# A relative-position bias table built as eight single rows and repeated 128 times by a memory-to-memory transfer, in a two-block decoder kernel

## The reference, cut to what matters

```
score = sum_h w_idx[q,h] * relu(q_idx[q,h] . k_idx[s])      # causal
sel   = top_k(score, 128)
dist  = t[:, None] - sel
logits = q_abs @ c_kv[sel] + rel_bias[rel_bucket(dist)]     # rel_bias is [32 buckets, 8 heads]
p = masked_softmax(logits, dist >= 0)
```

## Time and profile before

| | |
|---|---|
| profiled execution, its time | 2313.94 us |
| its span | 2312.1 us |
| TensorE busy | 2268.6 us, 98% |
| VectorE / ScalarE / GpSimd busy | 1128.8 (49%) / 870.7 (38%) / 389.9 us (17%) |
| mean granted TensorE clock | 0.987 |
| chain that ended last, by engine | PE 91%, ACT 3%, DVE 3%, DMA 1%, POOL 1% |

### The profile page before, as it was taken

How to read it: one execution, slowest core, us unless ns; L and a number is a source line. 1 busy time by engine, 2 the same in 40 slices (tenths; PEclk the granted TensorE clock), 3 DMA queues, 4 the chain that set the end, 5 groups by cost and what they waited for, 6 DMA issues and landing times.

```text
span 2312.1 us, 26070 instructions
## 1 busy us (share of the span) xinstructions
PE 2268.6 (98%) x10840; PEld 1842.9 (80%) x10840; DVE 1128.8 (49%) x1728; ACT 870.7 (38%) x1291; POOL 389.9 (17%) x339
## 2 busy tenths in 40 slices
PE   7999999999999999999999999999999999999998
PEld 5567888888876678888888878888888888888887
DVE  4974433434335645344345566554333446555553
ACT  5674222223225633122134485442322344233343
POOL 1431110112200012011032303332101211000020
PEclk9799999999999999999999999999999999999999
DMA  4203322322361022322345523224255333332331
GB/s 138 101 1 110 109 91 91 101 94 96 96 189 39 1 74 92 107 93 91 98 89 92 37 37 65 46 46 83 55 92 103 98 92 91 110 91 91 100 107 58
DMA packets 221955, 196.26 MB, mean 85 GB/s; under 512 B 7264, under 2 KB 215596, under 8 KB 221709
## 3 DMA queue, kind: packets, MB, share of 16 engines
q1 hardware_dynamic: 219820, 188.92, 31.1%
q0 software_dynamic: 1504, 5.51, 0.7%
q10 hardware_dynamic: 513, 0.17, 0.0%
HBM read 189.87 MB, written 4.72 MB: 84 GB/s over the span
## 4 chain that ended last, share of the span: by engine, by line
PE 91%; ACT 3%; DVE 3%; DMA 1%; POOL 1%; issue 0%; ACTq 0%; POOLq 0%
PE bank L540 24%; PE bank L542 24%; PE bank L541 24%; PE bank L2225 5%; PE bank L863 3%; PE bank L2411 2%; PE bank L1692 1%; PE bank L847 1%; PE bank L714 1%; PE bank L724 1%; PE bank L1309 1%; PE bank L2101 1%; DVE weight_lo L526 1%; PE bank L1510 0%; DVE hybrid_step L2340 0%
## 5 line engine op out<-in xcount | busy, mean ns | idle before, releaser
L540 PE MATMUL bank<-h_hi,weight_hi 128*128 128x512 f32 (+1 forms) x1568 | 616.4, 393 | 4.7 <-DVE h_lo L646 3.6
L542 PE MATMUL bank<-h_hi,weight_lo 128*128 128x512 f32 (+1 forms) x1568 | 612.5, 391 | 0.0
L541 PE MATMUL bank<-h_lo,weight_hi 128*128 128x512 f32 (+1 forms) x1568 | 612.1, 390 | 0.0
L526 DVE TENSOR_TENSOR weight_lo<-weight_raw,weight_hi 128x2048 fp32r<-128x2048 f32 (+3 forms) x181 | 382.9, 2116 | 363.0 <-ACT weight_hi L517 362.9
L517 ACT ACTIVATE weight_hi<-weight_raw 128x2048 fp32r<-128x2048 f32 (+2 forms) x182 | 319.8, 1758 | 335.9 <-PE bank L542 312.4
L540 PEld LDWEIGHTS bank<-h_hi,weight_hi 128*128 128x128 f32 (+1 forms) x1568 | 295.0, 188 | 68.7 <-issue 7.4
L542 PEld LDWEIGHTS bank<-h_hi,weight_lo 128*128 128x128 f32 (+1 forms) x1568 | 294.7, 188 | 63.3
L541 PEld LDWEIGHTS bank<-h_lo,weight_hi 128*128 128x128 f32 (+1 forms) x1568 | 294.9, 188 | 61.7 <-issue 0.2
L540 PE MATMUL bank<-hidden_hi,weight_hi 128*128 128x512 f32 x512 | 201.8, 394 | 0.0
L542 PE MATMUL bank<-hidden_hi,weight_lo 128*128 128x512 f32 x512 | 200.7, 392 | 0.0
L541 PE MATMUL bank<-hidden_lo,weight_hi 128*128 128x512 f32 x512 | 198.7, 388 | 0.0
(11 more groups left out here) (414 smaller groups left out, 3140.8 us busy)
## 6 DMA issues: line engine op xcount, KB each, us to landing
weight_raw<-in_w_down SPq DMA_DIRECT2D x40, 1024.0 KB, 5.1
weight_raw<-in_w_up SPq DMA_DIRECT2D x32, 1024.0 KB, 5.4
weight_raw<-in_w_up SPq DMA_DIRECT2D x44, 512.0 KB, 5.0
weight_raw<-in_w_in SPq DMA_DIRECT2D x20, 1024.0 KB, 8.8
weight_raw<-in_w_in SPq DMA_DIRECT2D x24, 512.0 KB, 6.7
weight_raw<-in_w_kv_shared SPq DMA_DIRECT2D x6, 1024.0 KB, 4.9
weight_raw<-in_w_branch SPq DMA_DIRECT2D x6, 1024.0 KB, 5.0
weight_raw<-in_a_w_o SPq DMA_DIRECT2D x4, 1024.0 KB, 5.7
```

Of the source, the lines that this page charges most:

```text
L526: dve.e.tensor_tensor(split_flat(v, 1), raw_flat(v), f32(split_flat(v, 0)), ALU.subtract).then_inc(*split.mark(("unit", v)))
L540: pe.e.matmul(o, w[0], x[0], start=start, stop=False)
L541: pe.e.matmul(o, w[0], x[1], start=False, stop=False)
L542: return pe.e.matmul(o, w[1], x[0], start=False, stop=stop)
```

## The change

`rel_bias` is no longer widened. Two matmuls (33 x 8 by 33 x 320) give all heads at once, one row a partition, early in the stage, right after `sums("kidx")`. ScalarE copies them to an 8 x 640 row buffer (20 KB). GpSimd writes that to a new DRAM tensor `bias_line`, waits for it, and starts one DRAM to DRAM transfer that reads each row 128 times and fills `skew` (2.6 MB), before it adds any score. The sheared read of `skew` is issued by GpSimd between the scores of tiles 2 and 3. The 16 matmuls, their copies, the eight sends and the waits on them are gone.

```diff
+        bias_line = nc.dram_tensor("bias_line", [HEADS, N_SHIFT], F32, kind="Internal")
-        bias_rows = [dsa_step(at, N_SHIFT) for at in (6 * T, 6 * T + N_SHIFT, 0, N_SHIFT)]
-        rel_wide = dsa_step(4 * T, HEADS, P)
+        bias_row = dsa_step(4 * T, N_SHIFT)
+        BIAS_PARTS = [(0, N_SHIFT // 2), (N_SHIFT // 2, N_SHIFT)]
@@ dsa_tensor
             sums("kidx", 64)
+            pe.wait_ge(*hot_in.when("hot"))
+            pe.wait_ge(*rel_in.when("rel"))
+            pe.wait_ge(*dsa.dve.when("neg"))
+            for n, (c0, c1) in enumerate(BIAS_PARTS):
+                bank = open_bank(pe, ("bias", n), (dsa.act, ("bias", n)))
+                pe.e.matmul(bank[0:HEADS, 0:c1 - c0], rel, one_hot[:, c0:c1], start=True, stop=True
+                            ).then_inc(*dsa.pe.mark(("bias", n)))
...
-            pe.wait_ge(*dsa.act.when("rel_wide"))
-            pe.wait_ge(*hot_in.when("hot"))
-            for h in range(HEADS):
-                for half in range(2):
-                    bank = open_bank(pe, ("bias", h, half), (dsa.act, ("bias", h, half)))
-                    pe.e.matmul(bank[:, 0:w], rel_wide[0:BUCKETS + 1, h, :], one_hot[:, half * w:half * w + w], start=True,
-                                stop=True).then_inc(*dsa.pe.mark(("bias", h, half)))
@@ dsa_scalar
                              ).then_inc(*dsa.act.mark(("w_rows",), ("kidx", "taken")))
+            for n, (c0, c1) in enumerate(BIAS_PARTS):
+                act.wait_ge(*dsa.pe.when("bias", n))
+                act.e.activation(bias_row[0:HEADS, c0:c1], banks.of("bias", n)[0:HEADS, 0:c1 - c0], ACT.Copy
+                                 ).then_inc(*dsa.act.mark(("bias", n)))
             scalar_fold(act, dsa, "kidx", latent_factors["kidx"], 1.0 / IDX_DIM)
...
-            act.e.activation(rel_wide[0:BUCKETS + 1], rel.unsqueeze(2).broadcast_to([BUCKETS + 1, HEADS, P]), ACT.Copy
-                             ).then_inc(*dsa.act.mark(("rel_wide",)))
...
-            for h in range(HEADS):
-                for half in range(2):
-                    act.wait_ge(*dsa.pe.when("bias", h, half))
-                    if h > 3:
-                        act.wait_ge(*skew_out[h % 4].when("skew", h - 4))
-                    act.e.activation(bias_rows[h % 4][:, half * w:half * w + w], banks.of("bias", h, half)[:, 0:w], ACT.Copy
-                                     ).then_inc(*dsa.act.mark(("bias", h, half)))
...
-                act.wait_ge(*skew_out[1].when("skew", HEADS - 3))
...
-                else:
-                    act.wait_ge(*skew_out[h].when("skew", HEADS - 4 + h))
@@ dsa_pool
             pool_squares(pool, dsa)
+            for n in range(2):
+                pool.wait_ge(*dsa.act.when("bias", n))
+            pool.e.dma_start(bias_line[:, :], bias_row[0:HEADS]).then_inc(*skew_out.mark(("line",), by=16))
+            pool.wait_ge(*skew_out.when("line"))
+            pool.e.dma_start(skew[:, :, :], bass.AP(tensor=bias_line, offset=0, ap=[[N_SHIFT, HEADS], [0, P], [1, N_SHIFT]])
+                             ).then_inc(*skew_out.mark(("skew",), by=16))
             for i in (2, 3):
...
+                if i == 2:
+                    sheared = bass.AP(tensor=skew, offset=P - 1, ap=[[N_SHIFT - 1, P], [P * N_SHIFT, HEADS], [1, T]])
+                    pool.wait_ge(*skew_out.when("skew"))
+                    pool.e.dma_start(bias[:, :, :], sheared).then_inc(*bias_in.mark(("bias",), by=16))
             uq = unit_at["uq", 0]
             pool.wait_ge(*rounded.when("unit", uq))
             pool.e.tensor_tensor(split_flat(uq, 1), raw_flat(uq), f32(split_flat(uq, 0)), ALU.subtract
                                  ).then_inc(*dsa.pool.mark(("unit", uq)))
-            for h in range(HEADS):
-                pool.wait_ge(*dsa.act.when("bias", h, 1))
-                pool.e.dma_start(skew[h], bias_rows[h % 4]).then_inc(*skew_out[h % 4].mark(("skew", h), by=16))
-            sheared = bass.AP(tensor=skew, offset=P - 1, ap=[[N_SHIFT - 1, P], [P * N_SHIFT, HEADS], [1, T]])
-            for n in range(4):
-                pool.wait_ge(*skew_out[n].when("skew", HEADS - 4 + n))
-            pool.e.dma_start(bias[:, :, :], sheared).then_inc(*bias_in.mark(("bias",), by=16))
```

More of the change, by code:

```diff
@@ L438, in build_program @@
         raw_in = [signal(f"weight_in{n}") for n in range(2 * N_RAW)]
-        skew_out = [signal(f"skew_out{n}") for n in range(4)]
-        bias_in, misc_in, out_done = signal("bias_in"), signal("misc_in"), signal("out_done")
+        skew_out, bias_in, misc_in, out_done = (signal(n) for n in ("skew_out", "bias_in", "misc_in", "out_done"))
         tile_full, rounded, split = signal("tile_full"), signal("weight_rounded"), signal("weight_split")
@@ L1048, in dsa_tensor @@
                                 start=True, stop=True).then_inc(*dsa.pe.mark(("score", i, h)))
-            w = N_SHIFT // 2
-            pe.wait_ge(*dsa.act.when("rel_wide"))
-            pe.wait_ge(*hot_in.when("hot"))
-            for h in range(HEADS):
-                for half in range(2):
-                    bank = open_bank(pe, ("bias", h, half), (dsa.act, ("bias", h, half)))
-                    pe.e.matmul(bank[:, 0:w], rel_wide[0:BUCKETS + 1, h, :], one_hot[:, half * w:half * w + w], start=True,
-                                stop=True).then_inc(*dsa.pe.mark(("bias", h, half)))
             u = unit_at["uk", 0]
@@ L1123, in dsa_scalar @@
                 act.e.activation(q_idxT[:, t, :], banks.of("q_idx", t), ACT.Copy).then_inc(*dsa.act.mark(("q_idx", t)))
-            act.wait_ge(*dsa.dve.when("neg"))
-            act.wait_ge(*rel_in.when("rel"))
-            act.e.activation(rel_wide[0:BUCKETS + 1], rel.unsqueeze(2).broadcast_to([BUCKETS + 1, HEADS, P]), ACT.Copy
-                             ).then_inc(*dsa.act.mark(("rel_wide",)))
             n = 0
```

## The result

Measured: 2316.17 us median (2313.39 to 2318.14, 21 runs) against 2312.71 (2310.22 to 2315.45, 21 runs); ratio 1.0015, 95% interval 1.001 to 1.0021. That is 3.5 us slower where 1.4 was forecast; within 0.2%. The profiled execution has a span of 2315.4 us.

What follows compares the result with a forecast made beforehand. VectorE's unbroken 64 us key search bounds the changed stretch; its 0.54 us delay is swallowed at L754, then L764 adds 1.4: 2313.94 + 1.4 = 2315.3, forecast 2315.2 us, within 0.2% (4.6 us); middle cases 2312.0 to 2318.5.

Steps and rivals of the forecast that it cites:

- The bound: VectorE's top-128 key search, 60.68 to 124.71 us, is unbroken and ends last before the attention.
- the freed `uq` path: Ahead of the attention: `uq` product 10 us earlier, worth 0; rival that this path was last, 2305.2 us, 5%.
- over 3: Slack of the `uq` path: first logit tile done near 121.6 us, over 3 us before it is used.
- no wait for another engine in it: VectorE's search for tiles 1 to 3, 64.03 us, was taken as never waiting for another engine.
- L540 of cq "near 92": Start of the `uq` product, behind L764 and its spread: near 92 us instead of 100.85.
- Added matmuls: Two bias matmuls ahead of L1033 delay TensorE's q_idx and first score by 0.84 us, 0.3 to 1.3.
- L1126: Widening of rel_bias on ScalarE ahead of the first relu: removing it gains 0.30 us, so the search begins 0.54 late.
- GpSimd's shift: Sheared-read issue and late scores move GpSimd's L1273 by 1.4 us, 0.9 to 2.0, delaying VectorE; rival no stall, 2314.1 us, 18%.
- L764 is about 1.9 us long: Midway in VectorE's search, L764 stalls until GpSimd's L1273 ends near 90.25 us, leaving 1.4 us later.
- The clock: TensorE's half-clock restart at the attention taken as equal in both kernels, bounds -1.5 to +1.5 us.
- The repeat: DRAM to DRAM copy lands between 60 and 70 us, holding nobody; late rivals 2317.9 us, 8%, and 2385, 4%.

Runs made afterwards that it cites:

- short-search pair: Kernel before and changed kernel, each with 8 instead of 16 key-search rounds for query tile 3: 2309.67 and 2302.99 us.
- a_again: The changed kernel run again with no edit: 2315.46 us against 2312.34 for the kernel before, ratio 1.0011.
- SyncE's share: Changed kernel with all three bias transfers issued by SyncE instead of GpSimd: 2315.39 us; with the bias matmuls also moved between q_idx tiles: 2314.27 us.
- the last variant: Changed kernel with bias matmuls behind tile 1's scores, transfers on SyncE, no extra tensor, fold on ScalarE, last scale step after tile 2's search: 2310.17 us.

## Why the prediction was right, and where its sizes were off

- **The bound** was right: no other engine opens a gap on VectorE in the search, and the short-search pair shows that the freed `uq` path is worth 0 until the search shrinks. Its slack was 2.7 us, not "over 3". And "no wait for another engine in it" holds for gaps alone: some 1.3 us of the search were GpSimd's hold inside L754 and L764 (1.17 and 0.48 us, where each takes 0.16 alone).
- **L540 of cq "near 92".** 92.48 in a_again and 94.63 in the first trace, in both 1.8 us after the end of L764 (90.64 and 92.78): the mechanism as told.
- **Added matmuls, "I take 0.84".** Measured 2.15 - 1.28 = 0.87 (L1041 in a_again against L1033). Right.
- **L1126, "0.30 us gained".** Wrong: 0.06. The first score comes 0.90 later in a_again and its relu 0.84. The relu starts 0.79 us after TensorE's first score does in before and 0.73 in the changed kernel; I had reckoned 0.43 for the score and nothing for what lies between it and the relu, so L1126 stood in the way much less than I took it to. So the search begins 0.87 late, not 0.54.
- **GpSimd's shift, "1.4 us".** L1272 starts 1.51 later (a_again, 40.10 against 38.59), L819 1.49. Right in size. "L764 is about 1.9 us long" was wrong: VectorE had been held at L1187 (1.10 us against 0.47) and came to L764 1.5 late itself. The sum did not suffer, because VectorE ends up as late as GpSimd at either place. SyncE's share, 0.55 to 0.58, is the GpSimd part measured alone.
- **The clock, "equal".** At the attention it was: it shows 0.50 from 130 to 134 us and 1.00 from 136 in before, 0.50 from 134 to 138 and 1.00 from 140 in the changed kernel. In q_idx, where I had not looked, it fell in half of the traces: 1.6 us when it does, some 0.8 on average. This term was missing.
- **Behind the attention** I had no term. Some 1.2 us more wait for cmp_w1_k came, of open cause, and the traces give some 1.0 back near 1385 us.
- **The repeat** landed at 69, inside "between 60 and 70".

By the traces the terms are 0.87 for the matmuls, 1.49 - 0.87 = 0.6 for GpSimd and 0.8 for the clock (1.6 in three of six), together 2.3 us. The measured difference is 3.5 us, and its interval reaches from 2.3 to 4.9; what makes up the other 1.2 us, if it is real, is open. The wait near 665 us has just that size, but the time from L819 to the end, equal in both, does not let it be counted. The 1.4 us of the forecast are the 1.5 of the front part without the clock.

Some of the hit was luck. The forecast added 1.4 us to 2313.84, the median of three runs; 21 runs put the kernel before at 2312.71. The forecast time, 2315.2, is therefore 1.0 us off, while the forecast change is 2.1 us off: it was 1.4 and became 3.5.

## What to carry to other kernels

Where two paths meet, read the last one from end to end before pricing anything on the other: an unbroken run of one engine's own work means that a wait removed elsewhere is worth nothing, and that small things ahead of the run's start cost their full size (here 0.87 us of matmuls). A sweep that shortens the last path (here by leaving out rounds) tells in one pair of runs what the other path's gain would be. Small VectorE instructions between long ones should stand where GpSimd is idle, or be given to ScalarE: that took 1.6 us off the search, by the trace alone.

## What was not expected of the hardware

- The long L754 agrees with the exclusive lock of the Trainium skill, page "SBUF — State Buffer", section "SBUF: two separate sides". L1187 (L1198 in before), a TENSOR_SCALAR of 128x256 with one SBUF tensor in, is held by GpSimd too: it took from 0.31 to 1.13 us and ended 0.15 us after a GpSimd addition's end in each of the fourteen traces, the last variant's included. The same section counts VectorE operations in a 2-port mode among those that lock; no view tells whether L1187 ran in one.
- Matmuls of 33 rows by 8 columns between other small ones preceded a fall of the granted clock from 1.00 to 0.50 in three of six traces, without TensorE having been idle. The cause is not shown.
- A DRAM to DRAM repeat of eight rows of 2.5 KB, 128 times each, ran at 210 GB/s at a DMA share of 0.51 and at 308 at 1.09.
